# Last of eight expert visits: all gate and up pieces ahead of the down pieces of block 1, and the sample rows' transposes ahead of the last two down pieces

## The reference

```python
def moe_swiglu(x, router, w_gate, w_up, w_down):
    ...
    for e in range(N_EXPERTS):
        y_e = swiglu(xt, w_gate[e], w_up[e], w_down[e])    # (silu(x @ wg) * (x @ wu)) @ wd
        y = y + combine[:, e:e + 1] * y_e.astype(jnp.float32)
...
x = layer_norm(ALPHA * x + f, ln2_g[l], ln2_b[l])
```

## Time and profile before

| | |
|---|---|
| Three executions | 1504.24, 1506.91, 1509.76 us |
| Median | 1506.91 us |
| Profiled execution, span | 1504.0 us; a time of its own beside the span is not shown for it, the lowest timed execution is 1504.24 us |
| PE, weight load, DVE, ACT busy | 94%, 77%, 89%, 74% of the span |
| Weights moved in the visits | some 410 GB/s in most slices of the second half |

### The profile page before, as it was taken

The page is one execution under the profiler, slowest core; times in us unless marked ns, Lnnn a source line. Parts: engine busy times, 40 slices in busy tenths (PEclk is TensorE's granted clock), DMA queues, the critical chain, the costliest instruction groups (busy, mean ns, idle before and its releaser), DMA issues.

```text
span 1504.0 us, 40039 instructions
## 1 busy us (share of the span) xinstructions
PE 1418.1 (94%) x17659; PEld 1161.2 (77%) x17659; DVE 1331.8 (89%) x1324; ACT 1107.7 (74%) x1036; POOL 111.0 (7%) x160
## 2 busy tenths in 40 slices
PE   7999999999999999899999999999999889898786
PEld 5888878888888788698687797788777776766663
DVE  4999987545569899899999999999999999999997
ACT  4797755444358676587897878888888888978884
POOL 2121014000043001200000000000000000000001
PEclk8999999999999999999999999999999999999898
DMA  9654466457554527879999999999999999999993
GB/s 316 237 168 155 162 235 219 141 183 236 171 180 141 172 87 270 345 304 380 405 413 392 412 411 397 411 409 394 411 407 410 412 406 411 411 401 410 411 396 132
DMA packets 141347, 464.86 MB, mean 309 GB/s; under 512 B 8234, under 2 KB 10410, under 8 KB 126800
## 3 DMA queue, kind: packets, MB, share of 16 engines
q1 hardware_dynamic: 138960, 457.21, 79.7%
q0 software_dynamic: 1920, 4.55, 1.0%
q10 hardware_dynamic: 288, 0.48, 0.1%
HBM read 460.79 MB, written 2.89 MB: 308 GB/s over the span
## 4 chain that ended last, share of the span: by engine, by line
PE 56%; DVE 29%; DMA 5%; issue 4%; ACT 3%; POOL 1%; SPq 1%; DVEq 0%; ACTq 0%
PE ps L859 17%; PE ps L860 17%; PE ps L861 17%; DVE w_lo L2274 13%; DVE w_lo L2277 6%; ACT w_hi L1655 2%; PE ps L972 2%; DMA x<-in_moe_w_gate 2%; DMA stage<-in_w_in 2%; DMA stage<-in_moe_w_up 1%; DVE w_lo L1746 1%; POOL x L786 1%; DVE arena L2292 1%; DVE arena L2312 1%; SPq L646 1%
## 5 line engine op out<-in xcount | busy, mean ns | idle before, releaser
L861 PE MATMUL ps<-arena,w_lo 128*128 128x128 f16 (+7 forms) x3952 | 568.9, 215 | 13.7 <-issue 13.6
L859 PE MATMUL ps<-arena,w_hi 128*128 128x128 f16 (+7 forms) x3952 | 569.1, 215 | 13.4 <-issue 6.6
L860 PE MATMUL ps<-arena,w_hi 128*128 128x128 f16 (+7 forms) x3952 | 569.1, 215 | 11.3 <-issue 11.3
L859 PEld LDWEIGHTS ps<-arena,w_hi 128*128 128x128 f16 x3952 | 388.3, 100 | 28.9 <-issue 16.9
L860 PEld LDWEIGHTS ps<-arena,w_hi 128*128 128x128 f16 x3952 | 388.2, 100 | 25.1 <-issue 16.5
L861 PEld LDWEIGHTS ps<-arena,w_lo 128*128 128x128 f16 x3952 | 388.2, 100 | 12.8 <-issue 6.9
L859 PE MATMUL ps<-xhl,w_hi 128*128 128x264 f16 x1120 | 312.0, 279 | 11.8 <-DVE w_lo L1746 4.6
L860 PE MATMUL ps<-xhl,w_hi 128*128 128x264 f16 x1120 | 311.9, 278 | 0.0
L861 PE MATMUL ps<-xhl,w_lo 128*128 128x264 f16 x1120 | 311.8, 278 | 0.0
L1746 DVE SCALAR_TENSOR_TENSOR w_lo<-stage,w_hi 128x2048 f16<-128x2048 f32 (+1 forms) x95 | 210.5, 2236 | 81.7 <-ACT w_hi L1352 81.4
L1352 ACT ACTIVATE w_hi<-stage 128x2048 f16<-128x2048 f32 (+1 forms) x95 | 174.5, 1853 | 88.1 <-PE ps L861 75.3
(11 more groups left out here) (345 smaller groups left out, 1937.1 us busy)
## 6 DMA issues: line engine op xcount, KB each, us to landing
stage<-in_moe_w_up SPq DMA_DIRECT2D x57, 1024.0 KB, 14.0
stage<-in_moe_w_down SPq DMA_DIRECT2D x56, 1024.0 KB, 14.4
stage<-in_w_in SPq DMA_DIRECT2D x43, 1024.0 KB, 5.5
mixer_only<-in_moe_w_up SPq DMA_DIRECT2D x39, 1024.0 KB, 13.1
stage<-in_moe_w_gate SPq DMA_DIRECT2D x33, 1024.0 KB, 8.4
arena<-in_moe_w_gate SPq DMA_DIRECT2D x32, 1024.0 KB, 13.4
mixer_only<-in_moe_w_gate SPq DMA_DIRECT2D x24, 1024.0 KB, 13.7
x<-in_moe_w_down SPq DMA_DIRECT2D x16, 1024.0 KB, 14.8
```

What stands on the lines that cost most here:

```text
L859: mm(out, ah, bh, start=start, stop=False, skip_group_check=True)
L860: mm(out, ah, bl, start=False, stop=False, skip_group_check=True)
L861: return mm(out, al, bh, start=False, stop=stop, skip_group_check=True)
```

## The change

The last visit gets an order of its own: g0 u0 g1 u1 d0 g2 u2 g3 u3 d1 d2 d3, so g3 is now 28 and 29, u3 30 and 31, d1 32 to 35; d2 and d3 keep their numbers. Loads, high parts, low parts and matmuls all follow it. Blocks 1, 2 and 3 now wait split at the same time, so in the last visit `hh` and `hl` are seen as eight chunks of 256 columns in place of four of 512 (`hidden_split`). `split_at` goes; the hidden split of block 3 stands at its regular place, which is now q = 32 and 33. PE turns residual group 1 after u3 (before: after d1) and group 2 after d2, ahead of d3 (before: after d3). No instruction is added or taken away on PE.

```diff
@@ -107,17 +107,25 @@
     return 2 * len(BLOCKS[b])
 
 
-def visit_order():
+def visit_order(last):
+
+    def whole(kind, b):
+        return [(kind, b, q) for q in range(n_pieces(b))]
 
     order = []
     for b in range(NB):
-        order += [(kind, b, q) for kind in "gu" for q in range(n_pieces(b))]
-        if b:
-            order += [("d", b - 1, q) for q in range(n_pieces(b - 1))]
-    return order + [("d", NB - 1, q) for q in range(n_pieces(NB - 1))]
-
-
-VISIT = len(visit_order())
+        order += whole("g", b) + whole("u", b)
+        if b and not (last and b > 1):
+            order += whole("d", b - 1)
+
+    return order + [p for b in range(1 if last else NB - 1, NB) for p in whole("d", b)]
+
+
+ORDERS = [visit_order(v == NE - 1) for v in range(NE)]
+VISIT = len(ORDERS[0])
+
+H_SLOTS = [8 if 2 * c <= CAP else 4 for c in CAPS]
+assert H_SLOTS[NE - 1] == 8
 ROUND = NE * VISIT
 assert VISIT % SLOTS == 0 and ROUND % RING == 0
 
...
@@ -590,14 +598,11 @@
                     .rearrange("a (k p) n -> (a p) k n", p=P)), k, width
 
 
-        def split_at(at, q, behind):
-
-
-            m = q - behind
-            last = max(i for i, p in enumerate(order) if p[0] == "u")
-            if at[1] == NE - 1 and m in (last - 2, last):
-                m = last if m == last - 2 else -1
-            return order[m] if m >= 0 else ("", 0, 0)
+        def piece_at(at, m):
+            return ORDERS[at[1]][m] if m >= 0 else ("", 0, 0)
+
+        def hidden_split(t, v):
+            return t.rearrange("p a b -> p (a b)").rearrange("p (a b) -> p a b", a=H_SLOTS[v])
 
         last_tile, part_no = {}, {}
 
...
@@ -1193,7 +1198,7 @@
 
 
                 cap = CAPS[at[1] % NE]
-                m = order.index((kind, blk, q))
+                m = ORDERS[at[1]].index((kind, blk, q))
                 slot = slot_of(m)
                 cs = BLOCKS[blk]
                 nk = KT // n_pieces(blk)
@@ -1226,10 +1231,11 @@
             def down(at, blk):
                 cap = CAPS[at[1] % NE]
                 for q in range(n_pieces(blk)):
-                    m = order.index(("d", blk, q))
+                    m = ORDERS[at[1]].index(("d", blk, q))
                     slot = slot_of(m)
                     end = blk == NB - 1 and q == n_pieces(blk) - 1
                     c = BLOCKS[blk][q // 2]
+                    h_at = c % H_SLOTS[at[1]]
                     pe.wait_ge(S["e_split"], so_far(at, NC, c + 2))
                     pe.wait_ge(S["lo_done"], so_far(at, VISIT, split(PRE) + m + 1))
                     for half in range(2):
@@ -1239,7 +1245,7 @@
                         for k in range(2):
                             f = 2 * (q % 2) + k
                             cols = slice(f * cap, (f + 1) * cap)
-                            t = mm3(ps[0:cap, b, :], hh[:, c % 4, cols], hl[:, c % 4, cols],
+                            t = mm3(ps[0:cap, b, :], hidden_split(hh, at[1])[:, h_at, cols], hidden_split(hl, at[1])[:, h_at, cols],
                                     wh(slot, k, half * 512, half * 512 + 512, D),
                                     wl(slot, k, half * 512, half * 512 + 512, D),
                                     c == 0 and f == 0, c == NC - 1 and f == 3)
@@ -1267,16 +1273,12 @@
                     t = mm(ps[0:cap, 7, 256:258], onehot[:, i, 0:cap], gsel[:, i, :], start=(i == 0), stop=(i == 2))
                 t.then_inc(bank_full[7], 1)
                 down(at, 0)
-                if at[1] == NE - 1:
-                    rows_in(at, 1)
+
+            def visit(at, first=False):
+                up_to_gather(at, first)
                 for blk in range(2, NB):
                     gate_up(at, blk)
                     down(at, blk - 1)
-                    if at[1] == NE - 1 and blk == 2:
-                        rows_in(at, 2)
-
-            def visit(at, first=False):
-                up_to_gather(at, first)
                 gather((at[0], at[1] + 1), at)
                 down(at, NB - 1)
 
@@ -1290,18 +1292,17 @@
                         mm(ps[0:n, TOKEN_BANK[i, h], k * P:(k + 1) * P], z[:, 4 * h + k, i * P:i * P + n], ident,
                            start=(k == 0), stop=False, skip_group_check=True)
 
-            def rows_in(at, blk):
-
-                if blk == 1:
-                    residual_rows(0, [tokens_added(at, 1), in_visit(bank_free, 7, at, 0)])
-                elif blk == 2:
-                    residual_rows(1, [columns_read(b, at, 2) for b in (1, 3)])
-
             def last_visit(at):
 
                 up_to_gather(at)
+                residual_rows(0, [tokens_added(at, 1), in_visit(bank_free, 7, at, 0)])
+                for blk in range(2, NB):
+                    gate_up(at, blk)
+                residual_rows(1, [columns_read(b, at, 2) for b in (1, 3)])
+                for blk in range(1, NB - 1):
+                    down(at, blk)
+                residual_rows(2, [columns_read(b, at, 3) for b in (0, 2)])
                 down(at, NB - 1)
-                residual_rows(2, [columns_read(b, at, 3) for b in (0, 2)])
 
             def token_rows_out(nv):
 
@@ -1640,9 +1641,9 @@
                 r, v = at
                 if m < 0:
                     v, m = v - 1, m + VISIT
-                kind, b, q = order[m]
-                if m in part_in_visit:
-                    return S["part_used"], so_far((r, v), NPART, PART0 + part_in_visit.index(m) + 1)
+                kind, b, q = ORDERS[v][m]
+                if m in parts_in[v]:
+                    return S["part_used"], so_far((r, v), NPART, PART0 + parts_in[v].index(m) + 1)
                 c = BLOCKS[b][-1]
                 bank_, i = {"g": (c % 2, c // 2), "u": (2 + c % 2, c // 2), "d": (5, 2)}[kind]
                 return in_visit(bank_full, bank_, (r, v), i)
@@ -1671,7 +1672,7 @@
                 for q in range(VISIT):
                     if q == 0:
                         y_hi(at)
-                    kind, blk, part = order[q - 1] if q else ("", 0, 0)
+                    kind, blk, part = piece_at(at, q - 1)
                     if kind == "g" and part == n_pieces(blk) - 1:
                         cs = BLOCKS[blk]
                         for b in range(len(cs)):
@@ -1679,11 +1680,12 @@
                         act.wait_ge(S["e_split"], so_far(at, NC, cs[0] + 1))
                         fn(silu_e[:, 0:len(cs), 0:4 * cap], ps[:, 0:len(cs), 0:4 * cap], ACT.Silu,
                            scale=1 / WS).then_inc(bank_free[0], 1)
-                    kind, blk, part = split_at(at, q, 2)
+                    kind, blk, part = piece_at(at, q - 2)
                     if kind == "u" and part == n_pieces(blk) - 1:
                         cs = BLOCKS[blk]
                         act.wait_ge(*columns_read(2, at, blk))
-                        fn(hh[:, cs[0] % 4:cs[0] % 4 + len(cs), 0:4 * cap], h_e[:, 0:len(cs), 0:4 * cap], ACT.Copy
+                        h_at = cs[0] % H_SLOTS[at[1]]
+                        fn(hidden_split(hh, at[1])[:, h_at:h_at + len(cs), 0:4 * cap], h_e[:, 0:len(cs), 0:4 * cap], ACT.Copy
                            ).then_inc(S["e_hi"], 1)
 
                     if at[1] < NE - 1 or q + SLOTS < VISIT:
@@ -2282,7 +2284,7 @@
                 for q in range(VISIT):
                     if q == 0:
                         y_lo(at)
-                    kind, blk, part = split_at(at, q, 1)
+                    kind, blk, part = piece_at(at, q - 1)
                     if kind == "u" and part == n_pieces(blk) - 1:
                         cs = BLOCKS[blk]
                         dve.wait_ge(*columns_read(0, at, blk))
@@ -2299,18 +2301,18 @@
                             V.tensor_copy(onehot_t[0:cap, :], ps[0:cap, 7, :].bitcast(F16)[:, 0:T])
                             V.tensor_reduce(gate_slot[0:cap, 0:1], ps[0:cap, 7, 256:258], X, ALU.add
                                             ).then_inc(bank_free[7], 1)
-                    kind, blk, part = order[q - 1] if q else ("", 0, 0)
+                    kind, blk, part = piece_at(at, q - 1)
                     if (kind, blk, part) == ("g", 1, n_pieces(1) - 1):
                         scatter_add(at, 1)
                     if (kind, blk, part) == ("d", 1, 0):
                         select((at[0], at[1] + 1))
-                    kind, blk, part = split_at(at, q, 2)
+                    kind, blk, part = piece_at(at, q - 2)
                     if kind == "u" and part == n_pieces(blk) - 1:
                         cs = BLOCKS[blk]
                         dve.wait_ge(S["e_hi"], so_far(at, NB, blk + 1))
-                        hs = slice(cs[0] % 4, cs[0] % 4 + len(cs))
-                        V.tensor_tensor(hl[:, hs, 0:4 * cap], h_e[:, 0:len(cs), 0:4 * cap], hh[:, hs, 0:4 * cap],
-                                        ALU.subtract).then_inc(S["e_split"], len(cs))
+                        hs = slice(cs[0] % H_SLOTS[at[1]], cs[0] % H_SLOTS[at[1]] + len(cs))
```

(20 more changed lines are left out.)

## The result

| | before | after |
|---|---|---|
| Median of five executions | 1504.24 us | 1514.04 us |
| Their range | 1502.63 to 1509.76 us | 1512.71 to 1515.77 us |
| Profiled execution, span | 1504.0 us | 1510.8 us |
| Its own time | not shown | 1512.71 us, the lowest of the five |
| PE, weight load, DVE, ACT busy | 94%, 77%, 89%, 74% | 94%, 77%, 88%, 73% |

The ratio is 1.0059 with a 95% interval of 1.0047 to 1.0071: the changed kernel is slower by some 9 us. (The median of before is lower than the one that stood ahead of the prediction, since two further executions, of 1504.02 and 1502.63 us, have joined the three.) A second set of five executions of the changed kernel, run beside the experiments, gave 1.0058 [1.0045 to 1.0071].

A forecast was written before the change was run, and what follows sets the result against it. Loads set the splitting pace; PE, busy without a gap, ends d3 at most 2.7 us above their floor. d3 ending 9.0 us later less 1.1 of tail gives +7.9 on 1506.9: 1514.8 us, range 1510.5 to 1518.5.

The forecast's parts named there:

- A: Last visit: u3 waits for `h_e`, then one stretch at half the clock; +7.9 us, 1514.8 us; chance 0.80.
- Where the wait would be, and its length: Between g3 and u3, PE idles 4.7 to 5.6 us until DVE's `h_e` of block 2 ends at 1461.5.
- the lines that I had drawn: Signs of being wrong: PE begins u3 before 1460, or d3 ends before 1492.
- The clock: In u3 behind the wait: one 3.41 us stretch at half clock, 1.5 us; bounds none, or a second stretch, 1.7 more.
- the eight-chunk view, `select` and the hidden split of block 3: In the last visit, set at nothing; the hidden split would cost 0.7 us each if its cover were gone.
- Group 2: Ahead of d3 it delays d3 by 1.84 us; behind d3, two DVE waits of 0.92 and 0.20 go, saving 1.1.
- The pauses: In gate and up pieces, code blocks some 6.3 us apart; next due at 1455.2 and 1461.5, within or beside the wait.
- B: At u3: `h_e` wait hidden, code still pauses PE until 1461.5; d3 ends 1492.1, +4.2, 1511 us; chance 0.11.
- C: PE runs g3 and u3 without any wait or pause, d3 ends 1488.6; +0.7, 1507.6 us; chance 0.06.
- D: Faster, at the floor set by the loads: d3 ends 1484.1, 2.7 us less, plus 1.1 of tail; 1503.1 us; chance 0.03.

The follow-up runs named there:

- repeat: The changed kernel unchanged, run again as yardstick beside the experiments: 1513.78 us, ratio 1.0058 to the kernel before; span 1512.0 us.
- first trace: The first profiled execution of the changed kernel, against the kernel before: span 1510.8 us, its own time 1512.71 us.
- the best order of this study: Kernel before with d0 and g2 alternating, `h_e` of block 2 and second half of `scatter_add(1)` two pieces earlier, `select` out of the loop: 1502.66 us, ratio 0.9987.
- the first experiment: Changed kernel with DVE making `h_e` of block 2 two pieces earlier: 1510.02 us, ratio 1.0037 to the kernel before.
- the second: Changed kernel with 16 idle matmuls of 512 columns into PSUM bank 1 between g3 and u3: 1510.83 us, ratio 1.0042 to the kernel before.

## Why the prediction was right

The forecast was 1514.8 us and +7.9 us on any base; measured were 1514.04 us, and +9.8 by the medians or 1.0059 x 1504.24, +8.9, by the ratio (interval +7.1 to +10.7). The named case, A, is what happened.

That the median came within 0.8 us is in part luck. The base, 1506.91 us, was 2.7 us above the median that five executions gave, and the step was 1 to 2 us too small; the two errors nearly cancel. The prediction also set the profiled execution, with its span of 1504.0 us, beside the lowest time. In the executions of this kernel for which both are on record the time is some 2 us above the span (1504.24 and 1502.2, for one), so by this estimate the profiled one took about 1506 us, over 1 us more than the median of 27 later ones (1504.79). The step was worked out from a trace that was itself a slow one of its kind, which hides part of it.

The terms, against the repeated trace, whose loads came at the times of the kernel before:

| step | forecast | repeat | first trace |
|---|---|---|---|
| g3 ends | 1455.9 to 1456.8 | 1455.87 | 1455.2 |
| u3 begins, behind `h_e` | 1461.5 | 1461.33 | 1459.37 |
| PE's wait | 4.7 to 5.6 | 5.46 | 4.18 |
| u3 | 4.3 | 4.90 | 5.09 |
| d1 and d2 | 20.9 | 20.91 | 20.84 |
| group 2 | 1.84 | 1.8 | 1.85 |
| d3 ends | 1495.8 | 1496.08 | 1494.78 |
| span | 1511.9 | 1512.0 | 1510.8 |

- **Where the wait would be, and its length.** Right: PE's arrival was moved, the release was not. In the first trace both ends lie 0.7 and 2.1 us earlier than forecast, which is scatter between executions: the loads of before's trace at this place were 2.3 us later (`h_e` at 1460.83 against 1458.54). It is enough to cross one of the lines that I had drawn: I had called myself wrong if u3 began before 1460, and in the first trace it began at 1459.37. The wait, its releaser and the idle PE were as forecast, and the repeat began u3 at 1461.33, so I count this as a line drawn too near to the scatter; the other line, d3 before 1492, was not crossed in either.
- **The clock.** The mechanism was right, its size was low. The step was "one stretch at half the clock", 1.5 us. u3 ran at 0.50 for the whole of its 5.09 us in the first trace, and group 1 behind it at 0.85; at the full clock the same 96 matmuls took 2.96 us. That is 2.1 us in u3 and (1.00 - 0.85) x 2.27 = 0.3 in group 1: 2.4 us, between the price I took and the upper bound of 3.2. In the repeat it is 1.9 us, all of it in u3.
- **No harm from the eight-chunk view, `select` and the hidden split of block 3.** Behind u3 PE waits for nobody before the end of d3, so it waits for none of them.
- **Group 2.** +1.84 on PE and -1.1 on DVE: both seen, the two waits to the hundredth. The tail as a whole became 1.3 us shorter, 0.2 more than the waits.
- **The pauses.** The block due at 1455.2, after 41 matmuls of g3, came there: as a pause of 1.0 us that ended at 1453.42, early by the 2 us of this execution, and of 0.70 us in the repeat; the one due at 1461.5 was covered by the wait. Without the wait it came at 1461.07. The Trainium skill, "Runtime: NRT & Kernel Launch", section "Instruction fetch mechanics", calls the cost of crossing a block of instructions "mostly hidden". That doesn't hold for this stretch: six pauses took 10.2 of 83 us.
- **The rivals.** B was made by an experiment and came within 0.5 us of its working. C needed both the wait and the pauses away. D's floor stands: it was 3.8 us below before, and the best order of this study is 2.2 us below.

What the 9 us are: some 3.8 for the wait and the clock behind it beyond what code would have held up anyway (the first experiment), of which the clock alone is 2 to 3 (the second), and about 5 that stay by the medians (3.7 by the two traces: d3 ends at 1491.76 in place of 1486.79, and the tail gives back 1.3). They stay since PE has 30 us of work left when u3 is done, and u3 is held by the pauses even when its wait is gone. What would be left without the pauses too was not run.

## What to carry to other kernels

When the loads set the pace, ask of each kind of piece whether PE is faster or slower on it than a load. Moving the cheap pieces (here 1.40 us against a load of 2.5) ahead makes PE idle now and saves work of the dear kind (2.62 us) for a time when the loads are over; mixed pieces keep both busy. Here mixing took pauses away but gave no time by itself; the fastest kernel also had VectorE's two waits moved. And before moving work ahead of a wait that never showed, find the instruction that ends it and its time in the trace: the wait's length is that time less the new arrival, and no sum over the moved work shows it. Its price can be less than its length, if something else stands next in line: here taking away 5.5 us of wait and the 1.9 us of half clock behind it gave back 3.8 us.

## What the runs showed of the hardware

- An idle TensorE costs more than its idle time. Behind 4.12 us without a matmul it was granted 0.50 for the next 5.09 us; 16 matmuls of 512 columns whose results nobody reads, put into the idle time, gave back 1.9 us inside u3 and 3.0 us by the medians. I had expected one stretch of 3.41 us as behind the 2.46 us pause.
- Small matmuls can run out of code. 128 matmuls of 64 columns take 3.9 us at the full clock, but the blocks came 6.1 to 6.4 us apart while the DMA engines were full. Each pause ended 2.2 to 2.6 us behind the start of a 16 KB packet on the instruction queue, and three of six pauses went when half the data was loaded.
